# Empty expert slots skipped, rows scattered by assignment, no zero fill, and w2's products in native fp32

## The reference, cut to what matters

```python
# gate (N, 2), expert (N, 2): top-1 group, top-2 experts in it; N = 1024 tokens, 32 experts
padded = (counts + MOE_BLOCK - 1) // MOE_BLOCK * MOE_BLOCK          # MOE_BLOCK = 128
...
def block_ffn(args):
    tok, e = args
    xb = xt[tok]
    hb = jax.nn.silu(xb @ w1[e]) * (xb @ w3[e])
    return hb @ w2[e]

out_buf = lax.map(block_ffn, (buf_tok.reshape(n_blocks, MOE_BLOCK), block_expert)).reshape(P, D)
y_assign = out_buf[dest].reshape(N, MOE_TOPK, D)
y = jnp.einsum('nk,nkd->nd', gate, y_assign)
```

## Time and profile before

| | |
|---|---|
| median of 3 runs | 2969.07 us (2966.35 to 2970.73) |
| the profiled execution | 2971.06 us |
| its span, first to last instruction | 2969.2 us |
| PE busy | 2599.6 us, 88% |
| DVE, ACT, POOL busy | 1203.7, 1177.7, 1036.8 us |
| DMA moved | 490.35 MB, mean 165 GB/s |
| mean granted clock of TensorE | 0.947 of full |

### The profile page before, as it was taken

The page is one execution under the profiler, slowest core; times in us unless marked ns, Lnnn a source line. Parts: engine busy times, 40 slices in busy tenths (PEclk is TensorE's granted clock), DMA queues, the critical chain, the costliest instruction groups (busy, mean ns, idle before and its releaser), DMA issues. The chain is left out here.

```text
span 2969.2 us, 31008 instructions
## 1 busy us (share of the span) xinstructions
PE 2599.6 (88%) x12104; PEld 2095.0 (71%) x12104; DVE 1203.7 (41%) x1637; ACT 1177.7 (40%) x1701; POOL 1036.8 (35%) x613
## 2 busy tenths in 40 slices
PE   6999978879899999899978799938977999999991
PEld 5888856668778878688867577835766777777770
DVE  4530027754122212223436522005135666666654
ACT  3212227754232122123214422214215777777762
POOL 3212203323212122313204532354103667666662
PEclk9999989999999999999979999979987999999995
DMA  4432145532211130422144333371444999999976
GB/s 152 145 119 92 53 102 138 130 93 86 85 50 43 64 107 29 118 75 92 57 136 141 107 121 110 132 289 57 148 186 178 374 375 374 384 374 373 375 293 248
DMA packets 173025, 490.35 MB, mean 165 GB/s; under 512 B 13936, under 2 KB 81552, under 8 KB 160208
## 3 DMA queue, kind: packets, MB, share of 16 engines
q1 hardware_dynamic: 117856, 382.62, 36.4%
q10 hardware_dynamic: 40080, 52.97, 4.9%
q0 software_dynamic: 14944, 52.78, 4.8%
HBM read 389.23 MB, written 99.09 MB: 164 GB/s over the span
## 5 line engine op out<-in xcount | busy, mean ns | idle before, releaser
L2524 ACT ACTIVATE ex_w_hi<-ex_w 128x2048 fp32r<-128x2048 f32 x198 | 378.7, 1916 | 169.8 <-DMA ex_w<-w 102.6
L2584 DVE TENSOR_TENSOR ex_w_lo<-ex_w,ex_w_hi 128x2048 fp32r<-128x2048 f32 x132 | 345.3, 2654 | 197.8 <-ACT ex_w_hi L2524 197.8
L227 POOL TENSOR_TENSOR p_w_lo<-w_raw,p_w_hi 128x512 fp32r<-128x512 f32 (+1 forms) x154 | 198.1, 1316 | 621.5 <-ACT p_w_hi L247 620.1
L2408 POOL TENSOR_TENSOR ex_w_lo<-ex_w,ex_w_hi 128x2048 fp32r<-128x2048 f32 x66 | 340.5, 5183 | 205.2 <-ACT ex_w_hi L2524 205.2
L227 POOL TENSOR_TENSOR p_w_lo_rest<-w_raw,p_w_hi_rest 128x512 fp32r<-128x512 f32 x94 | 123.1, 1343 | 275.0 <-ACT p_w_hi_rest L247 275.0
L366 PE MATMUL o_ps<-o_w_hi,o_m_hi 128*128 128x512 f32 x384 | 154.9, 403 | 19.8 <-POOL split_cols L1028 19.8
L368 PE MATMUL o_ps<-o_w_hi,split_cols 128*128 128x512 f32 x384 | 153.1, 399 | 0.0
L367 PE MATMUL o_ps<-o_w_lo,o_m_hi 128*128 128x512 f32 x384 | 152.9, 398 | 0.0
L366 PE MATMUL ex_pa<-ex_w_hi,ex_xT_hi 128*128 128x512 f32 x264 | 108.2, 410 | 31.4 <-issue 28.7
L1028 POOL TENSOR_TENSOR split_cols<-plain_cols,o_m_hi 128x1024 fp32r<-128x1024 f32 x24 | 57.3, 2391 | 214.0 <-ACT o_m_hi L1078 214.0
L366 PE MATMUL p_ps<-p_w_hi,hT_hi 128*128 128x512 f32 (+1 forms) x320 | 121.6, 380 | 2.6 <-PEq L279 2.6
(11 more groups left out here) (429 smaller groups left out, 6607.2 us busy)
## 6 DMA issues: line engine op xcount, KB each, us to landing
ex_w<-w SPq DMA_DIRECT2D x99, 2048.0 KB, 15.4
w_raw<-w_in SPq DMA_DIRECT2D x42, 1024.0 KB, 5.2
y_slots<-ex_y ACTq DMA_DIRECT2D x33, 512.0 KB, 12.0
y_slots<-xp_zero POOLq DMA_DIRECT2D x32, 512.0 KB, 16.8
att_k<-k_columns SPq DMA_DIRECT2D x48, 256.0 KB, 7.8
x_rows<-o_x SPq DMA_DIRECT2D x24, 512.0 KB, 2.6
w_raw<-w_out SPq DMA_DIRECT2D x8, 1024.0 KB, 9.7
qk_columns<-qk_y ACTq DMA_DIRECT2D x16, 512.0 KB, 2.6
```

Source lines behind the costliest of these rows:

```text
L227: emit(self.lo(n)[:, 0:w], self.half(n // (KC // 2), w)[:, n % (KC // 2), :], self.hi(n)[:, 0:w].bitcast(F32), ALU.subtract).then_inc(self ...
L2408: nc.gpsimd.tensor_tensor(w_lo[:, n % RING, :], raw_half(n), w_hi[:, n % RING, :].bitcast(F32), ALU.subtract).then_inc(down_lo, 1)
L2524: nc.scalar.activation(w_hi[:, n % RING, :], raw_half(n), ACT.Copy).then_inc(hi_done, 1)
L2584: nc.vector.tensor_tensor(w_lo[:, n % RING, :], raw_half(n), w_hi[:, n % RING, :].bitcast(F32), ALU.subtract).then_inc(up_lo, 1)
```

## The change

- `memory_projections`: the zero tile, its 32 stores and the wait for them are gone.
- `route`: the tokens' numbers are offset by 1 (and by 1024 for the second choice), so that an empty slot can be told. `slot_row` is the row of the assignment, token or token + 1024, and a number beyond all rows for an empty slot; `slot_token` is the token, and likewise beyond for an empty slot. `dest` is gone. POOL clears `xg` once.
- `experts`: the gather skips indices beyond the tokens (`bounds_check`). Rows of `y` are no longer stored as a block but scattered by POOL to `y_rows`, 2048 rows in the order of assignments, empty slots skipped.
- w2 isn't split: it has no pieces in the ring. PE multiplies `hT` (one fp32 tile, copied by DVE) by the raw matrix, 8 native fp32 matmuls in place of 24. The raw buffer of w2 is therefore in use until the products are done, and its next load waits for `y_done`.
- `combine`: plain loads of 128 rows of `y_rows`, half on SP's queue and half on ACT's, in place of the 16 gathers.

```diff
@@ load (ExpertWeights)
         if down:
             if b >= 2:
-                sp.wait_ge(down_lo, 2 * (b - 2) + 2)
+                sp.wait_ge(y_done, b - 1)
             sp.dma_start(self.w2s[j][:, :], self.w2[at].rearrange("e p n -> (e p) n")).then_inc(self.w2_in[j], 16)
@@ steps
             if b >= 1:
-                for half in range(2):
-                    yield n, "w2", b - 1, half
-                    n += 1
+                yield None, "w2", b - 1, 0
@@ experts, gpsimd
                     nc.gpsimd.indirect_dma_start(xg[:, b % 2, :], None, xn,
-                                                 bass.IndirectOffsetOnAxis(slot_token[:, b:b + 1].bitcast(U32), 0)
-                                                 ).then_inc(x_in[b % 2], 16)
+                                                 bass.IndirectOffsetOnAxis(slot_token[:, b:b + 1].bitcast(U32), 0),
+                                                 bounds_check=S - 1, oob_is_err=False).then_inc(x_in[b % 2], 16)
...
+                def scatter(b):
+                    pool.wait_ge(y_ready, b + 1)
+                    nc.gpsimd.indirect_dma_start(y_rows, bass.IndirectOffsetOnAxis(slot_row[:, b:b + 1].bitcast(U32), 0),
+                                                 y[:, b % 2, :], None, bounds_check=2 * S - 1, oob_is_err=False
+                                                 ).then_inc(y_out[b % 2], 16)
...
                 for n, m, b, half in steps():
-                    if n is not None and n + 3 in pieces and pieces[n + 3][0] == "w2":
-                        take_lo(n + 3)
                     if m == "turn_x" and b + 2 < NB:
                         gather(b + 2)
+                    if m == "w1" and half == 1 and b >= 2:
+                        scatter(b - 2)
@@ experts, tensor
-                def down(n, b, half):
-                    pe.wait_ge(down_lo, 2 * b + half + 1)
...
+                def down(b):
+                    pe.wait_ge(raw_in["w2"][b % 2], 16 * (b // 2) + 16)
+                    pe.wait_ge(h_kept, b + 1)
+                    if b >= 1:
+                        pe.wait_ge(y_ready, b)
+                    for k in range(KF):
                         for m in range(2):
...
+                            ins = pe.matmul(p_y[:, m * BANK:(m + 1) * BANK], hT[:, k * P:(k + 1) * P],
+                                            raws["w2"][b % 2][:, at], start=(k == 0), stop=(k == KF - 1))
+                    ins.then_inc(y_done, 1)
@@ experts, vector
                 def keep_h(b):
-                    dve.wait_ge(h_hi, b + 1)
-                    nc.vector.tensor_tensor(hT_lo[:, :], p_h[:, :], hT_hi[:, :].bitcast(F32), ALU.subtract).then_inc(h_lo, 1)
+                    dve.wait_ge(h_turned, b + 1)
+                    if b >= 1:
+                        dve.wait_ge(y_done, b)
+                    nc.vector.tensor_copy(hT[:, :], p_h[:, :]).then_inc(h_kept, 1)
...
                 for n, m, b, half in steps():
-                    if n is not None and n + 3 in pieces and pieces[n + 3][0] != "w2":
+                    if n is not None and n + 3 in pieces:
                         take_lo(n + 3)
@@ combine, sync and scalar
+                    sp.dma_start(y[:, t, 0, :], y_rows[t * P:(t + 1) * P, :]).then_inc(y_in[t], 16)
...
+                for t in range(NT):
+                    act.dma_start(y[:, t, 1, :], y_rows[S + t * P:S + (t + 1) * P, :]).then_inc(y_in[t], 16)
```

More of the change, by code:

```diff
@@ L2153, in _ @@
                 expert_weights.load(sp, 1)
+            @block.gpsimd
+            def _(pool):
+                nc.gpsimd.memset(xg[:, :, :], 0.0)
             @block.tensor
@@ L2285, in sems, with load @@
         return self.w1_in + self.w3_in + self.w2_in
-    def load(self, sp, b, up_lo=None, down_lo=None, up=True, down=True):
+    def load(self, sp, b, up_lo=None, y_done=None, up=True, down=True):
         if b < NE:
@@ L2385, in _ @@
                 for b in range(2, NB):
-                    weights.load(sp, b, up_lo, down_lo)
+                    weights.load(sp, b, up_lo, y_done)
                 def load(i):
@@ L2486, in _ @@
                     else:
-                        down(n, b, half)
+                        down(b)
                 def block_of_rest(i):
@@ L2538, in silu, with store @@
                     nc.scalar.activation(a[:, :], p_a[:, :], ACT.Silu).then_inc(a_ready, 1)
-                def store(b, n):
-                    act.wait_ge(used, n + 1)
+                def store(b):
+                    act.wait_ge(y_done, b + 1)
                     if b >= 2:
@@ L2558, in _ @@
                         keep_x(b)
-                    if m == "turn_h":
-                        keep_h(b)
-                    if m == "w2" and half == 1:
-                        store(b, n)
+                    if m == "w2":
+                        store(b)
                 act.sem_inc(r_free, 1)
@@ L2623, in _, with combine @@
                 over_rest(dve, block_of_rest)
-def combine(c, x3, y_slots, dest, gates, out):
+def combine(c, x3, y_rows, gates, out):
     nc, io = c.nc, c.io
@@ L2786, in build @@
             expert_weights.allocate(late, 1, up=True, down=True)
-            route(c, expert_weights, logits, bias, gates, dest, slot_token, extra_expert, n_rest)
-            experts(c, expert_weights, xn, y_slots, slot_token, n_rest)
-        combine(c, x3, y_slots, dest, gates, io["out"])
+            xg = late.enter_context(nc.sbuf_tensor("ex_x", [P, 2, D], F32))
+            route(c, expert_weights, logits, bias, gates, slot_token, slot_row, extra_expert, n_rest, xg)
+            experts(c, expert_weights, xn, y_rows, slot_token, slot_row, n_rest, xg)
+        combine(c, x3, y_rows, gates, io["out"])
 def kernel(**inputs):
```

97 lines of the change are left out of this document (35 added, 62 removed).

## The result

The changed kernel takes 3162.68 us, the median of 4 runs (3158.74 to 3166.7), beside 2969.32 (2966.35 to 2970.73) for the kernel before on the same chip. The ratio is 1.0653, with a 95% interval of 1.0634 to 1.0671: the change costs 193 us. The span of the profiled execution is 3161.3 us, 192.1 more than before.

A forecast was written before the change was run, and what follows sets the result against it. It took PE and the DMA engines as both almost full. Its terms, 227 (steps) + 0.4 (stage ends) + 2 (last scatter) - 39 (zero fill) - 4 (combine), gave +186.4 and 3156 us, with a range of 3100 to 3230.

The forecast's parts named there:

- the loop: Expert stage: products' end (Y), loads of w2 and w1, rounding, split, copy of hT, products, next Y; 27.1 us.
- The step: Expert stage, from one end of w2's products (Y) to the next: 27.1 us for 19.52, 227 over 30 steps.
- The clock, 1.7: TensorE's w2 products: after idling 5.7 us the clock falls, 1.7 us lost in each step, 51 in all.
- 12.7 + 0.6: Expert stage: w1 lands 12.7 us after w2's products end (Y) on an empty DMA, plus 0.6 for a scatter.
- rival 4: Expert stage: rows without a token are moved, not skipped; 0.6 us more a step, 3175 us; within the forecast's 0.68.
- The zero fill, -39: Before the memory attention: the wait of 42.1 us shrinks to a 3.1 hand-over; 39 gained, between 37 and 40.
- +1.3 for step 1: First step of the expert stage: w2's longer native fp32 products add 1.3 us.
- Combine, -4: Combine's first add waits less for its rows with direct loads: 4 us gained, between 0 and 8.
- the scatter's tail, +2: End of the expert stage: the last scatter replaces a store, 2 us more until landed, between 0 and 3.
- Rival 1: Expert stage: the load isn't waited for and TensorE bounds; step 19.6 us, total 2931 us; chance 0.05.
- Rival 2: Expert stage: clock doesn't fall or costs nothing; step 25.4 us, total 3105 us; chance 0.12.
- rival 3: Expert stage: w1 lands as late as before, 15.7 us, by competing traffic; step 29.5, total 3228 us; chance 0.11.

The follow-up runs named there:

- e1: Changed kernel, but SyncE issues the next block's w1 and w3 ahead of w2's load: 2918.69 us, ratio 0.9822.
- e4: Changed kernel with six native fp32 matmuls, results unread, ahead of the wait for hT in each step: 3134.93 us, ratio 1.0551.
- e8: Changed kernel with one more plain store of 0.52 MB per block on ScalarE's queue: 3223.03 us, ratio 1.0853.
- e10: Kernel of e5, but w1 and w3 are issued ahead of w2, and VectorE computes w2's lo halves instead of GpSimd: 2883.23 us, ratio 0.9705.
- e3: Changed kernel with the zero fill back at its place, into a scratch tensor that nothing reads: 3206.09 us, ratio 1.0796.
- e5: Changed kernel with w2's part undone: split, in the ring, three fp32r products, load waiting for GpSimd's splits: 2924.99 us, ratio 0.9844.
- e11: Kernel of e10 with SyncE's load order as before the change (w2, then the next block's w1 and w3): 2882.56 us, ratio 0.97.
- e9: Kernel of e5, but w1 and w3 go ahead of w2, and GpSimd computes only a quarter of w2's lo halves (products wrong): 2880.52 us, ratio 0.97.

## Why the prediction was right, and where it was not

The forecast was 3156 us and the time is 3162.7. Its mechanism is the one that the trace shows, and e1, which undoes the loop by issue order alone, moves the time by 244 us.

**The step, 27.1 forecast, 27.39 measured.** From Y to the rounding of w1: 0.05 + 13.3 forecast, 13.52 in the step shown. Rounding and hand-over: 1.97 and 1.94 (2619.47 to 2621.41). VectorE's split and the copy behind it: 2.96 forecast, 2.89 measured (2621.41 to 2624.30), and TensorE starts 0.1 later, as forecast. The products with drain and clock: 6.88 + 0.16 + 1.7 = 8.74, and 8.76 (2624.40 to 2633.16). In this step no term is off by more than 0.2 us. In the mean of the 30 the wait before the products is 6.0 us and the products take 8.8, since those of the first two steps take 9.8 and 9.3; that makes most of the 9 us between 227 and 236.

**The clock, 1.7.** In the step shown the granted clock is 0.50, the 1.2 GHz level, from the first pass to 2627.6, and 1.00 from 2628.5 on. Four passes start 0.85 us apart and the others 0.43, about 1.7 us lost, 8.72 against the 7.03 of e1. The sentence that the prediction quotes from the Trainium skill ("TensorE: Matmul & The Clock Gate", Part 1, What's actually happening), that "the ramp penalty is <1% of a typical kernel span", does not hold for this kernel: thirty ramps of 1.7 us are 1.6% of its span, and e4 got 40 us back between Y(1) and Y(31). TensorE idles here in every step.

**Traffic and landing.** w1 lands 13.2 us after its issue, which is 0.38 us after Y; I had 12.7 + 0.6 from Y. The price of bytes, 1.2 us for 0.52 MB by the earlier trace rows, was measured by e8 as 1.4. The skipped rows move no bytes: the DMA's software queue, which had 10.49 MB of gathers in 400 us before, has 11.8 MB in 600 us for gathers and scatters together, 0.54 MB a step for 0.52 of gathers alone. So rival 4 (the empty slots' rows are moved too) is out.

**Native fp32.** Sixteen passes of 0.43 us in e1 (7.03 us), and e1's step of 19.41 us against e10's 18.15: the 1.3 us a step that I gave as this edit's loss are 1.26.

**The zero fill, -39, and the stage's begin.** This step was mis-sized. I had kept 3.1 us for a hand-over that stays. In the changed kernel ScalarE waits 0.27 us at this place where the earlier trace rows had 42.11:

```profile
1965.17 1.28 ACT L2086 ACT_TABLE_LOAD   x1 [0.27 <-PEq L1916]
```

The 3.1 us between the last landing and the next stage belonged to the fill and went with it, so the term is 41.8. e3 gives 43 for the total. My +0.9 for the route and +1.3 for step 1 were too small: project_out and the route together take 2.9 us longer, and from the expert stage's first products to the first copy it is 2.2 us more. What hides them in the -41.4 of this stretch is the memory attention, 3.8 us shorter in the changed kernel. I had no term for that, and no run shows its cause.

**Combine, -4, and the scatter's tail, +2.** Both were mis-sized, and cancel. The first add waits 10.63 us for the rows, 1.23 less than in the earlier trace rows:

```profile
3122.78 1.29 DVE L2665 SCALAR_TENSOR_TENSOR cb_x<-cb_y,gates,cb_x 128x1024 f32<-128x1024 f32 x1 [10.63 <-DMA cb_y<-y_rows]
```

Direct loads come little sooner than gathers did. That ScalarE's queue and SyncE's ask for the other tiles at the same time may be why; no run tests it. I had taken the middle of 0 to 8 without a row for it. The tail from the last copy to combine's first instruction grew by 1.3 us. From the last copy to the first add the two kernels differ by 0.1 us.

**How much of the hit is luck.** Against the terms, the steps came out 9.2 us longer, the stretch up to the first copy 4.6 us shorter, the end from Y(31) to the last copy 1.1 us shorter (-2.9 for -1.8), and the scatter's tail and combine together 2.1 us longer. Errors of 17 us in all leave 5.6 in the sum. The mechanism and the step are shown; that the total is only 7 us off is in part cancellation.

**Rivals.** Rival 1 (the load isn't waited for, 2931) is refuted for this kernel, but it is e1: the forecast of a kernel bound by TensorE with native fp32, 2931, stands against 2919. The difference is mostly in the fill and in steps of 19.4 for 19.6 us: the 0.16 us of drain don't lengthen a step in which TensorE never waits (12.54 + 6.88 = 19.42). Rival 2 (no clock loss) is out by the windows, rival 3 (landing as late as before) by 13.2 us. That 15.7 us was the price of a gather and a store is what e8 makes likely: with one store more the landing is 14.6.

**What the prediction misread** without harm to its number is the bound of the kernel before. "Two resources are almost full at once" was true of the shares and wrong as a cause: TensorE at 23.2 of 25 us and the DMA engines at 0.92 were both held at this pace by a loop of GpSimd and VectorE. GpSimd's splits were called "worth nothing in time, since neither engine bounds", and they set the step. The long splits of VectorE in the earlier trace rows (4.4 us) were put down to GpSimd's work beside them and then not followed to who waits for them. Had the change kept w2's pieces and moved their splits to VectorE, this reading would have forecast no gain where e5 and e11 show 42 us. Whether the kernel before would gain as much from that move alone was not run. By estimate it would gain less: it moves 7.34 MB a step, which at 18.15 us would be some 404 GB/s, and no slice on the pages of these kernels (some 75 us each) is over 387.

## What to carry to other kernels

When a load's buffer is freed by the last work of a step, look at everything that stands behind this load on its queue, and follow it around until it meets the same work again: a loop that closes through a DMA landing costs the landing in every step, and issuing the other loads first can be the whole cure. Two engines with high shares are no proof of a bound: look for a closed chain of waits in which each link begins as soon as the one ahead of it ends, and then shorten one link, as e9 does, to see the step follow. And an operation given to an idle GpSimd can cost more than it saves when it keeps VectorE from starting, as the two splits did here.

## What the runs showed of the hardware

- VectorE's 128x2048 subtraction of two SBUF operands takes 2.29 us alone. Beside GpSimd's subtraction of the same form it does not start until that one ends: its record then shows up to 6.6 us, all of it counted as busy. GpSimd's takes 4.6 us alone and up to 5.9 where VectorE's was first.
- The gather (an indirect DMA) keeps GpSimd for 2.83 us in the kernel before, where it starts while one of VectorE's splits is under way and ends 0.8 us after that split. It takes 1.01 us in the changed kernel, where VectorE is idle at that time, and also in e10, beside VectorE's work on h and x, which has one operand in PSUM. That the split holds the gather up is likely by this; no run tests it alone.
- In e4 TensorE kept its clock over gaps of 0.65 to 2.13 us before w2's products, but for one of 1.99 us, where it lost it. In the changed kernel it lost it after each of the 30 gaps of 5.8 to 6.4 us, mostly for about four passes of 0.85 us (8.6 to 8.9 us for sixteen passes, twice 9.3 and 9.8, against 7.03 at full clock). In e8, after 7.2 to 8.2 us, sixteen passes took 8.5 to 10.1 us. What sets the size of the loss stays open.
- Native fp32 products of 128x512 come as two passes of 0.43 us, 0.86 together, and three fp32r products take 0.70.
